# An mLSTM + latent attention + MoE layer on one core: two homes for the left half of the expert weights, the right half in twelve pieces

## The reference, cut to what matters

```python
logits = (x2 @ w_router) + b_router
top_v, top_i = lax.top_k(logits, 4)
gates = jax.nn.softmax(top_v, axis=-1)
def expert_block(args):                    # one block of tokens of one expert e
    xb, e = args
    gu = xb @ w_gu[e] + b_gu[e]            # 1024 -> 2048
    gate = jnp.minimum(gu[:, :D_FF], 7.0)
    up = jnp.clip(gu[:, D_FF:], -7.0, 7.0)
    hid = (up + 1.0) * gate * jax.nn.sigmoid(1.702 * gate)
    return hid @ w_dn[e] + b_dn[e]         # 1024 -> 1024
```

## Time and profile before

| what | value |
|---|---|
| time, median of 3 runs | 1674.56 us (1670.5 to 1681.05) |
| span of the profiled execution | 1674.4 us |
| expert loop, first G0 to the end of the last D3 | 590.87 to 1651.72 us |
| blocks, experts | 39, 32 |
| PE busy | 1529.6 us (91%) |
| DMA moved | 478.17 MB, of it 461.47 MB on SP's queue |
| expert pieces loaded | 256 of `w_gate_up`, 128 of `w_down`, 1024 KB each |

### The profile page before, as it was taken

How to read it: one execution, slowest core, us unless ns; L and a number is a source line. 1 busy time by engine, 2 the same in 40 slices (tenths; PEclk the granted TensorE clock), 3 DMA queues, 4 the chain that set the end, 5 groups by cost and what they waited for, 6 DMA issues and landing times.

```text
span 1674.4 us, 20671 instructions
## 1 busy us (share of the span) xinstructions
PE 1529.6 (91%) x7178; PEld 703.5 (42%) x7179; DVE 354.8 (21%) x859; ACT 348.2 (21%) x672; POOL 125.6 (8%) x232
## 2 busy tenths in 40 slices
PE   8999999999999998887899988788999887998994
PEld 6676666666665433222233332222333222332331
DVE  2655422334211521010011010100111010101015
ACT  3535423534100211111111111101111110111111
POOL 0200000000000010000001000000101000010010
PEclk9999999999999999898999999889999997999996
DMA  7221232212464379999989899999899999579897
GB/s 262 92 79 57 95 109 78 76 51 101 139 237 166 134 288 409 416 419 407 417 311 415 353 415 417 412 411 421 312 368 393 412 414 402 215 309 411 324 409 265
DMA packets 92698, 478.17 MB, mean 286 GB/s; under 512 B 13096, under 2 KB 17053, under 8 KB 43507
## 3 DMA queue, kind: packets, MB, share of 16 engines
q1 hardware_dynamic: 84168, 461.47, 69.7%
q0 software_dynamic: 8096, 16.04, 2.9%
q10 hardware_dynamic: 394, 0.15, 0.0%
HBM read 472.06 MB, written 15.51 MB: 291 GB/s over the span
## 4 chain that ended last, share of the span: by engine, by line
PE 73%; DMA 18%; DVE 4%; issue 3%; SPq 1%; ACT 1%; ACTq 0%; DVEq 0%; POOLq 0%; POOL 0%
PE bank L613 28%; PE bank L1040 21%; DMA ring<-in_w_gate_up 17%; PE bank L1066 17%; PE bank L617 3%; PE bank L1046 1%; DVE r_kv L1494 1%; DVE r_v L1497 1%; PE bank L889 1%; DVE r_c L1497 1%; SPq L567 0%; PE bank L764 0%; DVE r_qk L1491 0%; SPq L574 0%; PE bank L884 0%
## 5 line engine op out<-in xcount | busy, mean ns | idle before, releaser
L1040 PE MATMUL bank<-ring,r_kv 128*64 128x512 f32 x2184 | 519.6, 623 | 89.7 <-DMA ring<-in_w_gate_up 89.0
L1040 PEld LDWEIGHTS bank<-ring,r_kv 128*64 128x64 f32 x2184 | 156.6, 142 | 397.7 <-issue 302.1
L1066 PE MATMUL bank<-ring,r_kv 128*64 128x512 f32 x1248 | 292.2, 612 | 0.7 <-ACT r_kv L1150 0.7
L613 PE MATMUL bank<-r_xt,ring 128*128 128x336 f32 x848 | 249.1, 448 | 1.1 <-ACT r_o L1150 0.9
L1491 DVE TENSOR_SCALAR r_kv<-bank 128x512 f32<-128x512 f32 (+1 forms) x80 | 55.0, 687 | 919.4 <-PE bank L1046 917.9
L613 PEld LDWEIGHTS bank<-r_xt,ring 128*128 128x128 f32 x848 | 158.1, 190 | 78.0 <-issue 5.6
L1066 PEld LDWEIGHTS bank<-ring,r_kv 128*64 128x64 f32 x1248 | 93.3, 144 | 198.2 <-issue 197.3
L1150 ACT ACTIVATE r_xt<-bank 128x512 f32<-128x512 f32 x39 | 23.3, 597 | 511.8 <-PE bank L1066 511.8
L1437 ACT ACTIVATE r_o<-r_kv 128x512 f32<-128x512 f32 x39 | 24.6, 631 | 318.2 <-DVE r_kv L1491 318.2
L617 PEld LDWEIGHTS bank<-const,r_v 64*128 64x128 f32 (+3 forms) x524 | 50.0, 157 | 77.2 <-DVE r_v L1497 43.9
L617 PE MATMUL bank<-const,r_v 64*128 64x64 f32 (+3 forms) x524 | 64.4, 259 | 10.6 <-DVE r_v L1497 10.4
(11 more groups left out here) (257 smaller groups left out, 958.2 us busy)
## 6 DMA issues: line engine op xcount, KB each, us to landing
ring<-in_w_gate_up SPq DMA_DIRECT2D x256, 1024.0 KB, 16.4
ring<-in_w_down SPq DMA_DIRECT2D x128, 1024.0 KB, 14.6
ring<-in_w_in SPq DMA_DIRECT2D x12, 2048.0 KB, 8.0
ring<-in_w_proj_b SPq DMA_DIRECT2D x2, 2048.0 KB, 7.8
ring<-in_w_proj_a SPq DMA_DIRECT2D x2, 2048.0 KB, 9.7
ring<-in_w_out SPq DMA_DIRECT2D x2, 2048.0 KB, 8.0
ring<-y_rows SPq DMA_DIRECT2D x8, 512.0 KB, 9.1
ring<-in_w_uq SPq DMA_DIRECT2D x2, 1152.0 KB, 9.2
```

The costliest lines, as they stand in the source:

```text
L613: ins = pe.matmul(out, l, r, start=(n == 0), stop=(n == len(pairs) - 1), **kw)
L1040: ins = pe.matmul(half(gate_bank if q < 2 else up_bank, q % 2), xg[:, k, :], w[:, 512 * q:512 * q + 512], start=False, stop=False, skip_gr ...
L1066: ins = pe.matmul(half(out_bank, t), hidT[:, 2 * (j % 2) + s, BLK * h:BLK * h + BLK], w[:, s, 512 * t:512 * t + 512], start=(j == 0 and s ...
```

## The change

The weights are laid out anew in DRAM on the host: `ex_left` and `ex_right` hold the left and right 512 columns of each pass's weights, `ex_left` in six pieces of 1 MB for each expert (two passes a piece), `ex_right` in twelve of 512 KB (one pass a piece). In SBUF `ring` grows from six to nine slots; buffers of the mixer that were tensors of their own become parts of the new slots, and small buffers of the loop move elsewhere. The left half gets two homes, one for even and one for odd experts; the right half has one.

PE's passes, their order and their number of matmuls stay. A pass now waits for a right piece, and every second pass for a left piece as well. The address of the left operand comes from a register (`own`), since the home depends on the expert's parity.

SP loads expert 0 and the left half of expert 1 before the loop. In the loop it issues, for each expert, the twelve right pieces behind the same waits as before, and then the six left pieces of the expert after that, in a row. The final gain vector (`g_fin_b`) is loaded after the router's last step.

```diff
-        ring = sb("ring", [128, 6 * SLOT])
+        ring = sb("ring", [128, 9 * SLOT])
...
+        left = [ring[:, EVEN:EVEN + HALF], ring[:, ODD:ODD + HALF]]
+        right = ring[:, 0:HALF]
...
+            filled(sp, "ya", 7)
+            for n in range(2):
+                left_first(0, n)
+                right_first(2 * n)
+                right_first(2 * n + 1)
+            for n in range(2):
+                left_first(1, n)
+            filled(sp, "out", 2, 0)
+            for n in range(4, 8):
+                right_first(n)
+            filled(sp, "out", 2, 1)
+            for n in range(8, 12):
+                right_first(n)
+            for n in (4, 5):
+                left_first(1, n)
+            filled(sp, "lg", 2)
+            for n in (2, 3):
+                left_first(1, n)
...
+            def left_next(e, half):
+                for n in range(6):
+                    sp.wait_ge(left_in[n], 16 * e)
+                    sp.dma_start(piece(half, n), ex_left[n, :, bass.ds(e, 1), :].rearrange("p a f -> p (a f)")
+                                 ).then_inc(left_in[n], 16)
+
+            def right_next(e, before):
+                for n in range(12):
+                    if n < 8:
+                        sp.wait_ge(m_up, before * 8 + n + 1)
+                    else:
+                        sp.wait_ge(m_down, before * 4 + n - 7)
+                    sp.dma_start(right_piece(n), ex_right[n, :, bass.ds(e, 1), :].rearrange("p a f -> p (a f)")
+                                 ).then_inc(right_in[n], 16)
+
+            with sp.Fori(0, NE // 2 - 1) as pair:
+                odd = sp.snap(2 * pair + 1)
+                even = sp.snap(2 * pair + 2)
+                right_next(odd, sp.value_load(firsti[0:1, bass.ds(odd, 1)].bitcast(I32), min_val=0, max_val=MAXB))
+                left_next(even, left[0])
+                right_next(even, sp.value_load(firsti[0:1, bass.ds(even, 1)].bitcast(I32), min_val=0, max_val=MAXB))
+                left_next(sp.snap(2 * pair + 3), left[1])
+            right_next(NE - 1, sp.value_load(firsti[0:1, NE - 1:NE].bitcast(I32), min_val=0, max_val=MAXB))
...
+            def halves_in(n, e):
+
+                if n % 2 == 0:
+                    pe.wait_ge(left_in[n // 2], 16 * e + 16)
+                pe.wait_ge(right_in[n], 16 * e + 16)
+
+            def gate_up(k, e, own):
+
+                halves_in(k, e)
+                for bank_, q, done in ((gate_bank, 0, m_gate), (up_bank, 1, m_up)):
+                    at = 1024 * k + 512 * q
+                    for t, w in ((0, own), (1, right)):
+                        ins = pe.matmul(half(bank_, t), xg[:, k, :], w[:, at:at + 512], start=False, stop=(k == 7),
+                                        skip_group_check=True)
+                    if k == 7 or q == 1:
+                        ins.then_inc(done, 1)
...
+                own = ring[:, bass.ds(pe.snap(e % 2 * (ODD - EVEN) + EVEN), HALF)]
+                own1 = ring[:, bass.ds(pe.snap(e1 % 2 * (ODD - EVEN) + EVEN), HALF)]
```

More of the change, by code:

```diff
@@ L91 @@
 SLOT = 4096
-UPSLOT, DNSLOT = [4, 5, 3, 0], [1, 2]
+HALF = 6 * 2048
+EVEN, ODD = 3 * SLOT, 6 * SLOT
 def by_chunk(pair, h, src):
@@ L340, in build, with piece, right_piece @@
         pick = small(BLK)
[L341 to L359, removed]
+        inslot = r3(usig[:, 0:12 * BLK], 12)
+        spread = r3(r_c[:, 3072:3072 + 12 * NB1], 12)
+        prod = usig[:, 768:1152].rearrange("p (t k e) -> p t k e", t=3, k=4)
+        prod_g = r_c[:, 3072:3456].rearrange("p (t k e) -> p t k e", t=3, k=4)
+        cmp6 = r_c[:, 3920:3920 + NE * 6].rearrange("p (e n) -> p e n", n=6)
+        xg = r3(r_qk[:, 0:512], 8)
+        hidT = r3(r_qk[:, 512:1024], 4)
+        gt = r_qk[:, 1024:1536]
+        up = r_qk[:, 1536:2048]
+        sg = r_qk[:, 2048:2560]
+        hid = r_qk[:, 2560:3072]
+        gateT = r_c[0:NE, 3584:3584 + NT]
+        xrow = usig[0:BLK, 0:1024]
+        yrow = r_c[:, 3072:3584]
+        left = [ring[:, EVEN:EVEN + HALF], ring[:, ODD:ODD + HALF]]
+        right = ring[:, 0:HALF]
+        def piece(half, n):
+            return half[:, 2048 * n:2048 * n + 2048]
+        def right_piece(n):
+            return right[:, 1024 * n:1024 * n + 1024]
         def y_turn(t, r):
@@ L395, in build @@
         slot_in = [sem(f"slot_in{n}") for n in range(4)]
-        up_in = [sem(f"up_in{n}") for n in range(8)]
-        dn_in = [sem(f"dn_in{n}") for n in range(4)]
+        left_in = [sem(f"left_in{n}") for n in range(6)]
+        right_in = [sem(f"right_in{n}") for n in range(12)]
+        ld_fin = sem("ld_fin")
         (rms_v, rms_s, xn_ready, cq_ready, kv_ready, kr_ready, low_v, low_s, conv_done, sig_ready, qk_ready,
@@ L546, in _, with left_first, right_first @@
             sp.dma_start(bd_rows, i["b_down"][0]).then_inc(ld_late, 16)
-            for k in range(4):
-                sp.dma_start(up_w(k), gu[:, 0, k, :]).then_inc(up_in[k], 16)
+            def left_first(e, n):
+                sp.dma_start(piece(left[e % 2], n), ex_left[n, :, e, :]).then_inc(left_in[n], 16)
+            def right_first(n):
+                sp.dma_start(right_piece(n), ex_right[n, :, 0, :]).then_inc(right_in[n], 16)
+            for n in range(2, 6):
+                left_first(0, n)
             filled(sp, "g", 3)
@@ L565, in _ @@
-            sp.wait_ge(moe_tab, 1)
[L566 to L575, removed]
+            filled(sp, "ya", 7)
@@ L1055, in hidden_turned, with down @@
                         at = 128 * (2 * j + s)
-                        ins = turn(ht_bank[:, at:at + 128], hid[:, 256 * j + s:256 * j + 256:2])
+                        ins = turn(ht_bank[:, at:at + 128], hid[:, at:at + 128])
                 ins.then_inc(m_turn, 1)
[L1059 to L1063, removed]
+            def down(j, e, own):
+                halves_in(8 + j, e)
                 for s in range(2):
[L1065 to L1068, removed]
+                    at = 8192 + 512 * (2 * j + s)
+                    for t, w in ((0, own), (1, right)):
+                        ins = pe.matmul(half(out_bank, t), hidT[:, 2 * (j % 2) + s, BLK * (j // 2):BLK * (j // 2) + BLK],
+                                        w[:, at:at + 512], start=(j == 0 and s == 0), stop=(j == 3 and s == 1),
+                                        skip_group_check=True)
                 ins.then_inc(m_down, 1)
@@ L1095, in _ @@
                         down_bias(banks[n], n // 2, n % 2).then_inc(bd_full, 1)
-                gate_up(k, 0)
+                gate_up(k, 0, left[0])
             pe.wait_ge(bd_free, 6)
@@ L1108, in _ @@
                 pe.wait_ge(m_xg, b + 2)
-                gate_up(0, e1)
+                gate_up(0, e1, own1)
                 pe.wait_ge(m_hidT, b + 1)
                 pe.wait_ge(yrow_free, b + 1)
[L1112 to L1116, removed]
+                down(0, e, own)
+                down(1, e, own)
+                down(2, e, own)
+                gate_up(1, e1, own1)
+                down(3, e, own)
                 for k in range(2, 8):
-                    gate_up(k, e1)
+                    gate_up(k, e1, own1)
             pe.wait_ge(m_xrow, 16 * nb + 16)
@@ L1125, in _ @@
             for j in range(4):
-                down(j, NE - 1)
+                down(j, NE - 1, left[1])
         @block.scalar
@@ L2072, with expert_half @@
         ("s_m", (1, 1, 4)), ("s_conv", (1, 1, 3, 2048))]
+def expert_half(w_gate_up, w_down, side, n):
+    gu = w_gate_up[0].reshape(NE, 8 // n, n, 128, 2, 2, 512)[:, :, :, :, :, side].transpose(0, 1, 3, 2, 4, 5)
+    dn = w_down[0].reshape(NE, 4 // n, 2 * n, 128, 2, 512)[:, :, :, :, side].transpose(0, 1, 3, 2, 4)
+    return np.concatenate([gu.reshape(NE, 8 // n, 128, 1024 * n), dn.reshape(NE, 4 // n, 128, 1024 * n)], axis=1)
 def kernel(**inputs):
@@ L2082 @@
         arrays["in_" + name] = np.ascontiguousarray(inputs[name])
+    for side, (name, n) in enumerate((("left", 2), ("right", 1))):
+        arrays["in_ex_" + name] = expert_half(np.asarray(inputs["w_gate_up"]), np.asarray(inputs["w_down"]), side, n)
     arrays["in_consts"] = constants()
```

64 lines of the change are left out of this document (30 added, 34 removed).

## The result

| | before | after |
|---|---|---|
| time, median | 1673.19 us (1670.5 to 1681.05) | 1805.4 us (1803.47 to 1809.89) |
| span of the profiled execution | 1674.4 us | 1808.1 us |
| start of the second block, of the last block | 614.10, 1617.23 us | 613.71, 1748.63 us |
| PE's waits for weights in the loop | 89.0 us in 17 | 208.1 us in 24 |

The change makes the kernel slower: ratio 1.0788, interval [1.0757, 1.0819]. Of the 133.7 us between the two spans, 131.8 lie between the start of the second block and that of the last (1134.9 us, before 1003.1).

A forecast was written before the change was run, and what follows sets the result against it. It saw single-expert blocks bound by DMA (31.2 us against 23.7 of PE), multi-block experts by PE. With the change, 37 periods sum to 1104.6 us against 1003.1, so 1674.4 + 101.5 = 1776 us, range 1735 to 1820.

The forecast's parts named there:

- D3's issue, the last R piece, all of L, the first R piece: From start to start: down pass D3, last right piece, left half, first right piece; 33.3 us after a wait, else 31.2.
- L: The left half of an expert's weights, 6 MB, put at 15.6 us of transfer in the chain between block starts.
- both of its own bounds: Allowances on the sum: +14 for gathers during the left half's transfer, +-9 for when D3's piece is issued.
- rival 5: PE's left operand: register addresses cost PE in full, 61 us more, 1837 us; chance 7%.
- the 2.6 us a MB: DMA time taken for the weight pieces in the loop, giving 1.3 us a right piece and 15.6 us a left half.
- both gathers falling into L's transfer, 0.6 us in 24 periods, +14: Upper bound on the forecast for gathers that move during the left half's transfer in the loop.
- I take 0: PE's left operand address from a register was costed at nothing; if none were hidden, 61 us.
- The queue runs dry for about 2 us: In the loop, queued right pieces give out before the next are issued, so the chain sets the period.
- Rival 1: The queue hides the chain in 17 single-expert periods, which stay at 31.2 us: 1740 us; chance 8%.
- The DMA share: How full the DMA engines are between 640 and 822 us; to fall from 1.01 to about 0.94.
- Rival 4: Each right piece pays its own latency, 29 us more in 24 periods, near 2470 us; chance 1%.
- Rival 3: The left half's second home gives a real lead, so DMA work alone counts in the loop: 1589 us; chance 6%.

The follow-up runs named there:

- experiment 1: Against the changed kernel, each left piece is issued directly behind the right piece of the pass that frees its home: 1679.72 us, ratio 1.0018 to the kernel before.
- experiment 4: Against the changed kernel, scatters, and gathers from the third block on, are plain 4 KB DMAs, not indirect 256 KB ones: 1778.05 us, ratio 1.0606 to the kernel before.
- Experiment 3: Against the changed kernel, PE reads the right half at a fixed address for both column halves, both waits kept: 1801.97 us, ratio 1.0763 to the kernel before.
- experiment 5: Against the kernel before, 18 MB of homes as one ring of 1 MB pieces issued in order of use, fixed addresses: 1625.16 us, ratio 0.9692.

## Why the prediction was right

*The mechanism held.* "D3's issue, the last R piece, all of L, the first R piece" is what the chain of waits shows, and experiment 1 shows it to be the cause by taking it away. The waits are 24, as foreseen, though longer (8.7 us and not 7.5, 208.1 in all and not 180), and no start at 23.7 us is left outside the experts with more blocks and their followers' first starts:

```profile
854.56 3.68 PE bank L1087 x8
...
880.66 1.87 PE bank L1087 x8
...
904.25 1.87 PE bank L1087 x8
...
919.36 15.99 DMA ring<-in_ex_right
...
935.65 3.68 PE bank L1087 x8
```

The two-block expert starts at 854.56 and its second block 26.10 us later (predicted 25.7), its follower after 23.59 (23.7), and the one after that only after 31.40 (31.2): L could not leave before the follower's D3. Before, that last step was 23.7 us.

*The size was 30 us short.* The time of 1805.4 us lies above the forecast with both of its own bounds (1776 + 14 + 9 = 1799). It is inside the range only through the room kept for rival 5, which did not happen, so that the range holds is partly luck. Predicted +101.5 us between second and last start, measured +131.8:

| periods | number | predicted us | mean us | adds up to |
|---|---|---|---|---|
| single expert, start out of a wait | 17 | 33.3 | 34.68 | +23.4 |
| single expert, start without a wait | 7 | 31.2 | 31.9 | +4.8 |
| first block of an expert with more | 6 | 25.7 | 26.16 | +2.8 |
| start that PE sets | 7 | 23.7 | 23.59 | -0.7 |

The terms of the first line, in the mean over its periods: D3's issue 12.9 us after the start (predicted 12.7), the lone right piece 3.55 from issue to landing (2.4 + 1.3 = 3.7), and from there to the landing of the first right piece 17.9 (predicted 15.6 + 1.3 = 16.9), then 0.30 to the start (predicted nothing). In the second line D3's issue is the 10.6 us of the prediction.

- *The term that was mis-sized is L, with the first right piece behind it: 17.9 us for 16.9.* At the pace of queued pieces (2.48 us a left one, 1.28 a right one) it would be 16.2, so the 2.6 us a MB, taken from periods of before with the gathers' share in them, held 0.7 for this traffic, and the bound "both gathers falling into L's transfer, 0.6 us in 24 periods, +14" 0.6 more. Gather and scatter do fall into L: its second and sixth piece land 2.85 and 3.42 us after their neighbours, and 2.52 and 2.50 in experiment 4. The price there, 25.4 us in 24 waits or 1.06 each, is 0.4 over the share and within the bound. The other 0.6 us stand in experiment 4 as well (16.8 for 16.2): there the first left piece lands 3.0 us after the lone right one, not 2.48. Nothing in the sum stood for that, and its cause stays open. So the agreement of experiment 4 with the predicted 1104.6 us is partly luck.
- *The step from landing to start was missing.* It is 0.30 us against 0.05 before (804.50 + 17.64 to 822.19): 6 us in 24. Experiment 3 puts 0.16 of it down to the register address. The rest goes with the second wait: the ring of experiment 5, with one wait and fixed addresses, is at 0.05 (779.23 + 27.54 to 806.82); that wait was not tested by itself.
- *"I take 0" for the register address* was right for passes (23.59 us in every block that PE sets, 23.7 before) and for what it adds to D3's time, short by 4 us for the starts.
- *"The queue runs dry for about 2 us"*: about 2.8. Rival 1 needed it to be full.
- *The DMA share* was to fall to about 0.94 between 640 and 822 us and is 0.96, with 371 GB/s in place of 413.
- *Right pieces 1.3 us apart*: queued, they land 1.28 us apart, and left pieces 2.48. Rival 4, the latency paid by each piece, did not happen. The 2.0 us that the prediction sets beside it from the Trainium skill, page "DMA: Bandwidth & Descriptors", section "Anatomy of one DMA — SWDGE (gpsimd) path", are given there for DMAs issued from GpSimd; these are issued by SP, and a lone one comes to 2.4 in the prediction's sum.
- *Before and after the loop* nothing was costed: the second block starts 0.4 us earlier, and the down passes at the end take 9.65 us where they took 10.12. From the last start to the end it is 2.3 us longer all the same (1808.1 less 1748.63, before 1674.4 less 1617.23); the last block now starts out of a wait.

```profile
1748.63 3.68 PE bank L1087 x8
...
1775.94 9.65 PE bank L1107 x32
```

Rival 3, a second home that works as a real lead, put the kernel at 1589 us by DMA work alone. Experiment 5 is the nearest to it that was built, and comes to 1625. Its gain is real, but needs another order, not only another home.

## What to carry to other kernels

Here a second buffer gave no lead by itself; it depended on the order in which its loads were issued. The pieces land in the order of their issue, so whatever is fetched early stands ahead of what is needed next, and here 6 MB of early weights cost 7.9%. So ask for every load what is ahead of it in the queue when it becomes urgent, and write the period as a chain (release, issue, everything queued ahead, its own transfer). The same memory as a ring in the order of use gained 3.1% on the kernel before, with idle DMA time of the PE-bound blocks used for the DMA-bound ones.

## What the hardware showed that I had not expected

- A DMA of 512 KB in rows of 4 KB, queued behind others, lands 1.28 us after its neighbour; 1 MB in rows of 8 KB takes 2.48 us. That is 2.56 and 2.48 us a MB, so the shorter rows cost 3% at most.
- A matmul with an operand address from a register costs nothing while PE is busy ahead of it (23.59 us a block with and without), and 0.16 us where the first pass waits for a landing.
- A late start costs more than its wait. Three stretches of the kernel after, in the columns of the earlier trace rows: the end of a wait, the first pass behind it, and a first pass without a wait.

```profile
674.00:680.90 6.90, 0.00 (x0) 0.00 (x0) 0.00 (x0) 0.00 (x0) 0.00 (x0) 0.59 1.01 371
681.24:684.92 3.68, 3.68 (x10) 1.24 (x12) 0.00 (x0) 0.00 (x0) 0.00 (x0) 0.50 1.03 410
...
880.66:882.52 1.86, 1.86 (x10) 0.70 (x12) 0.00 (x0) 0.60 (x1) 0.35 (x1) 1.00 1.02 432
```

PE did nothing for the 6.90 us, the clock granted to it was 0.59 in the mean, and the pass behind the wait ran at 0.50, which is the 1.2 GHz level, for 3.68 us; without a wait ahead it ran at 1.00 (2.4 GHz) and took 1.87. That is 1.8 us on top of the wait, and the passes behind it are slower too (D0 to D2 take 5.46 us after it, 5.15 at 882.52): a whole block that starts out of a wait takes 26.2 us where PE alone sets it, and one that doesn't 23.59. There are 24 such starts, where the kernel before has 17.
